# One core, two transformer blocks: indexer scores read by pairs, one pair of score matmuls moved into the first gate tile's product

## The reference, cut to what matters

```python
logits = jnp.einsum('bqhd,bsd->bqhs', qi, ik)
score = jnp.einsum('bqhs,bqh->bqs', jax.nn.relu(logits), wi)
score = jnp.where(admissible[None], score, -jnp.inf)
_, sel = lax.top_k(score, topk)
...
q = (rms_norm(bq, q_norm_g[l]) @ w_uq[l]).reshape(b, p, B_HEADS, B_HEAD_DIM)
gates = jax.nn.sigmoid((gates + b_gates[l]).astype(jnp.float32))
```

## Time and profile before

| | |
|---|---|
| median of 3 runs | 1500.18 us (1499.02 to 1501.77) |
| the profiled execution, its own time | 1499.58 us |
| its span, first to last instruction | 1497.9 us |
| PE busy | 1477.7 us, 99% of the span |
| DVE, ACT, POOL busy | 957.0, 605.1, 221.2 us |
| mean granted TensorE clock | 0.999 of full |

### The profile page before, as it was taken

One profiled execution on the slowest core, in us unless ns is written; L12 is line 12 of the kernel. 1 busy time (PEld: TensorE's weight loads), 2 busy tenths in 40 slices (PEclk: granted clock), 3 DMA queues, 4 the chain that ended last, 5 costly groups with the idle time before them and its releaser, 6 DMA issues.

```text
span 1497.9 us, 21903 instructions
## 1 busy us (share of the span) xinstructions
PE 1477.7 (99%) x8042; PEld 1233.0 (82%) x8042; DVE 957.0 (64%) x1707; ACT 605.1 (40%) x1061; POOL 221.2 (15%) x194
## 2 busy tenths in 40 slices
PE   8999999999999999999999999999999999999998
PEld 7867776878788888898898777777787888888987
DVE  6668897565795587377854372424667855873865
ACT  5235436534443243244511374444344433432434
POOL 2013324340000000000003663322400000000000
PEclk9999999999999999999999999999999999999999
DMA  7624320033333333332323202121333333333322
GB/s 174 152 65 146 117 57 1 23 104 99 98 99 99 101 97 99 98 104 71 107 85 84 56 2 85 57 64 36 102 95 99 99 99 112 89 95 98 113 70 100
DMA packets 250309, 132.99 MB, mean 89 GB/s; under 512 B 21225, under 2 KB 247653, under 8 KB 250222
## 3 DMA queue, kind: packets, MB, share of 16 engines
q1 hardware_dynamic: 247998, 123.92, 29.2%
q0 software_dynamic: 2144, 7.77, 1.8%
q10 hardware_dynamic: 80, 0.14, 0.0%
HBM read 129.67 MB, written 6.38 MB: 91 GB/s over the span
## 4 chain that ended last, share of the span: by engine, by line
PE 91%; DVE 5%; DMA 1%; issue 1%; ACT 1%; POOL 0%; SPq 0%; DVEq 0%; ACTq 0%
PE psL L2050 50%; PE psS L2073 12%; PE psL L2236 11%; PE psS L2050 5%; PE psT L2245 2%; PE psL L2371 1%; PE psS L2541 1%; PE psL L2496 1%; PE psS L2344 1%; PE psS L2519 1%; PE psS L2475 1%; DVE acc L1479 1%; PE psS L2286 1%; DVE st L1478 1%; PE psS L2476 0%
## 5 line engine op out<-in xcount | busy, mean ns | idle before, releaser
L775 ACT ACTIVATE wh<-stage 128x1024 fp32r<-128x1024 f32 (+3 forms) x232 | 225.4, 971 | 366.2 <-PE psL L2050 260.0
L2050 PE MATMUL psL<-hn,wh 128*128 128x512 f32 x1104 | 347.9, 397 | 0.4 <-DVE ft L1733 0.4
L2050 PEld LDWEIGHTS psL<-hn,wh 128*128 128x128 f32 x1104 | 204.8, 188 | 50.3 <-issue 3.7
L1208 DVE TENSOR_TENSOR wl<-stage,wh 128x1024 fp32r<-128x1024 f32 (+1 forms) x157 | 187.6, 1195 | 78.9 <-ACT wh L775 78.5
L2050 PE MATMUL psL<-hn,wl 128*128 128x512 f32 x552 | 217.1, 393 | 0.0
L2050 PE MATMUL psL<-hid,wh 128*128 128x512 f32 x680 | 209.6, 390 | 1.4 <-DVE wl L1208 1.4
L636 POOL TENSOR_TENSOR wl<-stage,wh 128x1024 fp32r<-128x1024 f32 (+2 forms) x75 | 140.0, 1867 | 278.5 <-ACT wh L775 278.5
L2236 PE MATMUL psL<-hn,wh 128*128 128x512 f32 x496 | 166.9, 418 | 2.2 <-DVE tmp L1468 2.0
L2050 PEld LDWEIGHTS psL<-hid,wh 128*128 128x128 f32 x680 | 127.4, 188 | 28.9 <-DVE wl L1208 2.2
L2050 PE MATMUL psL<-hid,wl 128*128 128x512 f32 x340 | 132.3, 389 | 0.0
L2050 PEld LDWEIGHTS psL<-hn,wl 128*128 128x128 f32 x552 | 103.8, 188 | 23.5
(11 more groups left out here) (438 smaller groups left out, 2644.3 us busy)
## 6 DMA issues: line engine op xcount, KB each, us to landing
stage<-in_w_in SPq DMA_DIRECT2D x54, 512.0 KB, 3.8
stage<-in_w_ffn_gate SPq DMA_DIRECT2D x22, 512.0 KB, 3.8
stage<-in_w_ffn_up SPq DMA_DIRECT2D x22, 512.0 KB, 3.8
stage<-in_w_ff_gate SPq DMA_DIRECT2D x22, 512.0 KB, 3.8
stage<-in_w_ff_up SPq DMA_DIRECT2D x22, 512.0 KB, 3.8
stage<-in_w_out SPq DMA_DIRECT2D x16, 512.0 KB, 4.0
stage<-in_w_ffn_down SPq DMA_DIRECT2D x16, 512.0 KB, 4.0
stage<-in_w_ff_down SPq DMA_DIRECT2D x16, 512.0 KB, 4.1
```

What stands on the lines that cost most here:

```text
L775: act.activation(wh[:, b, 0:n], stage[:, b, 0:n], ACT.Copy).then_inc(hi[b], 1)
L1208: v.tensor_tensor(wl[:, b, 0:n], stage[:, b, 0:n], wh[:, b, 0:n].bitcast(F32), ALU.subtract).then_inc(lo[b], 1)
L2050: ins = pe.matmul(dst, w[:, b, k * P:(k + 1) * P], x[:, part, k, c0:c1], start=k + n == 0, stop=k == kc - 1 and n == 2)
```

## The change

On ACT the relus are grouped by pairs: relu 9 comes ahead of `high` uq1 (1,0), relu 11 ahead of `high` gates1 (0,0), relu 13 ahead of `high` gates1 (0,1). On DVE additions 10 and 11 move by one place: addition 10 comes behind the eviction of uq1 (1,0) rather than ahead of it, addition 11 behind the eviction of uq1 (1,1). On PE `logits(6)` no longer stands between uq1 (1,1) and the gate tile; it is made inside gates1 (0,0), ahead of chunk 1. Nothing is added or removed in the arithmetic.

```diff
             relu_of(4, 8)
             high("uq1", 0, 1)
-            relu_of(8, 9)
+            relu_of(8, 10)
             high("uq1", 1, 0)
-            relu_of(9, 10)
             high("uq1", 1, 1)
-            relu_of(10, 11)
+            relu_of(10, 12)
             high("gates1", 0, 0)
-            relu_of(11, 13)
+            relu_of(12, 14)
             high("gates1", 0, 1)
-            relu_of(13, 16)
+            relu_of(14, 16)
...
             take_scaled("uq1", 0, 1, qT[:, 1, :], sq[:], QSCALE)
-            add_logits(9, 11)
+            add_logits(9, 10)
             take_scaled("uq1", 1, 0, qT[:, 2, :], sq[:], QSCALE)
+            add_logits(10, 11)
             low("gates1", 0, 0, ())
-            add_logits(11, 12)
             take_scaled("uq1", 1, 1, qT[:, 3, :], sq[:], QSCALE)
-            add_logits(12, 16)
+            add_logits(11, 16)
...
             product("uq1", 1, 1, bqg)
-            logits(6)()
...
-            product("gates1", 0, 0, hn, between={(0, 5): logits(7)})
+            product("gates1", 0, 0, hn, between={(0, 1): logits(6), (0, 5): logits(7)})
             pe.wait_ge(lg_taken, 4 * NB)
```

## The result

| | before | changed |
|---|---|---|
| median, 12 executions each | 1499.39 us | 1503.0 us (1501.06 to 1505.53) |
| the profiled execution | 1499.58 us, span 1497.9 | 1505.53 us, span 1503.8 |
| mean granted clock in it | 0.999 | 0.995 |

The ratio is 1.0019, 95% interval 1.0011 to 1.0027: slower by 2.8 us, or 1.6 to 4.0; the two medians differ by 3.6 us. The new median lies inside the predicted range of 1499.9 to 1503.8, but not at the forecast of 1501.5. That it meets rival 1's 1503.0 to the tenth is luck: rival 1 put its 2.81 us on the median of three executions, 1500.18, and over twelve the kernel before has 1499.39.

A forecast was written before the change was run, and what follows sets the result against it. PE, 99% busy, was taken as the bound, with the gate weights ending last ahead of the gate product. Pair 6 inside it (1.17) plus later weights (0.10) made 1.27 us, on the median 1500.18: 1501.5 us, range 1499.9 to 1503.8.

The forecast's parts named there:

- the forecast of 1501.5: Whole kernel: 1.27 us later at the first score of w1, put on the median of 1500.18; chance 0.47.
- rival 1: Ahead of the gate product: the 2.20 us gap drops the clock, costing 1.54 us more, 1503.0 us; chance 0.33.
- The path: Uq1 (1,0) split through gate load to gate product: later weights start the product 0.10 us later (0.03 to 0.17).
- the split's delay: POOL's `low` of uq1 (1,0), behind relu 9 on ACT: ends 0.26 to 0.40 us late, taken as 0.33.
- the lower bound: POOL's `low` of uq1 (1,0): 0.74 us long of 0.74 to 0.88, ending 0.26 us late of 0.26 to 0.40.
- The covers: POOL's later `low` of gates1 (0,1), about 2 us of cover left, and DVE's moved additions: no cost.
- the inserted pair: Pair 6 between chunks of the gate product on PE: costs 1.17 us, all on the path.
- a border between 1.34 and 2.00 us: PE gaps: whether the clock falls is decided by a gap length somewhere between these two values.
- Rival 2: At 216.67, where PE waits 2.00 us for DVE: up to all 1.27 us absorbed, 1500.2 us; chance 0.09.
- Rival 3: Ahead of the gate product: the gap closes as meant, a gain of 0.9 us, 1499.3 us; chance 0.05.

The follow-up runs named there:

- the gap filled: The changed kernel plus two extra matmuls on PE between uq1 (1,1) and the gate product, run twice: ratios to before 1.0011 and 1.0006.
- pair only: The kernel before with only pair 6 moved into the gate product, ACT and DVE as they were: ratio to before 1.0013 (1.0004 to 1.0022).
- split first: The kernel before with ACT's `high` of uq1 (1,0) put ahead of relu 8, run twice: ratios to before 0.9990 and 0.9997.
- relus only: The changed kernel with pair 6 put back ahead of the gate product: ratio to before 1.0004 (0.9994 to 1.0013).
- the second profile of the changed kernel: The unmodified changed kernel timed again beside the kernel before: ratio to before 1.0023 (1.0014 to 1.0033).
- the third changed run: The unmodified changed kernel timed a third time beside the kernel before: ratio to before 1.0021 (1.0012 to 1.0030).
- relu 9 back: The changed kernel with relu 9 back behind the split of uq1 (1,0) on ACT: ratio to before 1.0024 (1.0015 to 1.0033).
- the second filled one: Second run of the changed kernel with two extra matmuls ahead of the gate product: ratio to before 1.0006, median 1501.66 us.
- changed, split first: The changed kernel with ACT's `high` of uq1 (1,0) put ahead of relus 8 and 9: ratio to before 1.0005 (0.9995 to 1.0016).
- the first filled one: First run of the changed kernel with two extra matmuls ahead of the gate product: ratio to before 1.0011, median 1500.61 us.

## Why the prediction was right, and where it was off

**The path.** Right in kind at each step. PE idles for DVE's `low` and no longer for a relu. The landing moved by the split's delay: `high` started at 103.14 (forecast 103.0), `low` at 104.23 ended at 105.46 (105.34), PE began at 105.52 (105.38); 0.16 of this is the later start of the whole stretch. POOL's `low`, 0.88 us long before, where it ran beside DVE's addition of 97.45 to 98.09, now starts behind that addition and took 0.74, the lower bound; PE's wait grew by 0.25, the lower bound too. The load then took 3.84 us, and other executions varied by some tenths.

**The covers held.** POOL's `low` of gates1 (0,1) moved by 3.7 us, of which 1 is the clock's doing, and PE had no wait at the first quarter. DVE finished the additions at 115.50, 0.10 us behind the start of PE's first scores of w1, and still had 0.37 us to wait for them, as these rows of the changed kernel show against the earlier trace rows; POOL's, against the earlier trace rows, stands below them:

```profile
110.13 0.77 DVE L1438 SCALAR_TENSOR_TENSOR acc<-relu,iwn,acc 128x528 f32<-128x528 f32 x1
113.86 1.64 DVE L1438 SCALAR_TENSOR_TENSOR acc<-relu,iwn,acc 128x528 f32<-128x528 f32 x2 [2.96 <-ACT relu L844]
...
116.08 0.37 DVE L1484 CUSTOM_DVE_ANT_0 W3a<-psS,biasA,nsink 128x144 f32<-128x144 f32 x1 [0.37 <-PE psS L2271]
```

```profile
110.75 2.38 POOL L636 TENSOR_TENSOR wl<-stage,wh 128x1024 fp32r<-128x1024 f32 x1 [10.77 <-ACT wh L775]
```

The addition that had taken 2.50 us beside POOL takes 0.77 now, and it buys nothing: DVE idles 2.96 us right behind it.

**A term mis-sized: the inserted pair.** Forecast 1.17, measured 1.30 (8.33 - 7.03). I counted from the last start of a chunk to the first of the next and left out that the first matmuls behind the pair also follow each other more slowly. With it, the sum without the clock is 1.4: the changed kernel's product started 8.44 after relu 8, and 8.44 + 8.33 - 15.39 = 1.38, to 1.60 with the product starts of its other two executions. Forecast 1.27.

**The choice between forecast and rival 1.** This is where the forecast was wrong. The range held because it had been drawn wide enough for rival 1. All three profiled executions of the changed kernel show the fall. That it comes in most of the 36 is an estimate, since the mean clock of an execution doesn't tell where it fell. 0.61 of them ran at 0.996 or less, 0.35 with the gap filled. If each of these had the late fall of about 3 us that is described below, that makes 0.8 of the 2.1 us between the two kernels and leaves 1.3 for the fall at 106, some eight tenths of its price. It doesn't come in every one: five of the 36 ended below 1501.5 us. The price was right: 9.88 us for the product against 8.33 in "pair only" is 1.55, as forecast (1.54). Together 1.38 + 1.55 = 2.93 us, which is what the first score of w1 shows. I gave 0.33 to it although its gap of 2.20 us was longer than the one seen to lower the clock. The chances should have been the other way round. Nor is there a border between 1.34 and 2.00 us that decides, as I wrote there: gaps of 2.13 and 2.28 us kept the clock. (The gap of 2.00 us isn't the one other large one either: PE waits 2.86 and 1.29 us in its first 5 us, ahead of all products.)

**What rival 1 had wrong: a fall costs only where PE is the bound.** I took its price from the fall at 216.67, as if that one had cost the kernel 1.54 us too. The runs show that it hadn't. From that gap's end to the first `wuk` product (L2301) are 16.05 us before, and 16.09 and 15.99 in the two "split first" profiles, which fell there too. In the nine profiles that kept the clock they are 15.73 to 15.78. So this fall costs 0.3 us. Where the clock stays, PE runs into the next wait for DVE. PE's timeline in "pair only":

```profile
217.16 0.70 PE L2235 MATMUL psL<-hn,wh 128*128 128x512 f32 x2 [2.00 <-DVE tmp L1468]
...
225.34 0.70 PE L2235 MATMUL psL<-hn,wh 128*128 128x512 f32 x2 [1.09 <-DVE tmp L1468]
```

In the kernel before, with the clock down, the second wait doesn't exist; it is hidden in the slow matmuls. At 106 nothing but PE is late, and all 1.55 us count.

**Rivals 2 and 3.** Rival 2 falls: from the first score of w1 to L2301 are 120.41 us before (112.31 to 232.72) and 120.10 in the changed kernel (115.40 to 235.50), and those 0.3 are the fall above. Rival 3 falls with "relus only": the gap had another cause than the relu.

**What the profiled execution adds.** Its 5.9 us over before are more than 2.93 - 0.3. The rest, about 3 us, comes later, in two places of the span where the clock was down in it and not in before:

```profile
748.00:750.00 2.00, 2.00 (x11) 2.00 (x11) 1.66 (x11) 0.00 (x0) 0.00 (x0) 0.50 0.87 251
858.00:860.00 2.00, 2.00 (x8) 1.20 (x6) 1.51 (x5) 1.06 (x4) 1.49 (x2) 0.50 0.00 0
```

These waits of PE can serve as marks, first before, then changed:

```profile
742.62 1.95 PE L2111 MATMUL psT<-ones,sqacc 128*128 128x1 f32 x16 [0.24 <-DVE sqacc L1617]
850.87 0.71 PE L2475 MATMUL psS<-kaT,qaT 64*128 64x264 f32 x2 [0.80 <-DVE negm L1485]
745.58 1.95 PE L2110 MATMUL psT<-ones,sqacc 128*128 128x1 f32 x16 [0.24 <-DVE sqacc L1616]
854.76 0.71 PE L2473 MATMUL psS<-kaT,qaT 64*128 64x264 f32 x2 [0.80 <-DVE negm L1484]
```

The fall at 748 costs 0.9 us: between the marks are 108.25 us before and 109.18 in the changed kernel. It is in nine of the twelve profiles (109.16 to 109.20) and missing in just the three that fell at 216 (108.25 to 108.28); why it is one or the other isn't shown. The fall at 857 costs about 3.

From L2301 to the end it took 1503.8 - 235.5 = 1268.3 us, and 1500.5 - 235.2 = 1265.3 in the second profile of the changed kernel, which kept the clock there. The fall at 857 is in the profiles of the third changed run too, and of "relus only", "relu 9 back", the second filled one and "changed, split first", and not in those of before, "pair only", the first filled one and both "split first". So it comes in some executions and not in others of one kernel, and it is why two of them differ by 3 us. Whether the change makes it more frequent is open. The profiles lean that way (none of four with the old order of the relus, six of eight with the new), but the kernel before seems to have it too: the six profiles with this fall ran at a mean clock of 0.995 or 0.996 and the six without at 0.997 to 0.999, and 0.33 of before's 91 executions ran at 0.996 or less, some 2 us above its median. The difference of the means, 3.7 us over all and 3.5 within each comparison, is 0.7 or 0.6 above what the stretch explains, with errors of 0.16 and 0.26 us for the two means.

## What to carry to other kernels

A wait on the critical engine that seems to have one cause often has a second, nearly as late. Before moving work out of a gap, work out when the next item could start without it; here the gap was 1.34 us and only 0.2 of it could be had by the rows, 0.3 by the run. The pair in that gap was nearly free, and moved out of it, it cost its full 1.30. The place to gain was, by the traces, one step up the chain: a small split on ACT that fed the load of the late tile, put into idle time. Before explaining the difference of two single executions, look through the whole span for falls of the clock that one of them has and the other hasn't.

## What the runs showed of the hardware

The clock's answer to a gap isn't a fixed function of its length. In 12 profiles the same wait of 2.00 us at 215 to 220 us was followed by a fall in three (before and both "split first") and by none in nine. Ahead of the gate product, gaps of 2.26, 2.32 and 2.49 us were followed by one, gaps of 2.13 and 2.28 were not, nor were seven gaps from 0.34 to 1.60 ahead of the product or of pair 6. Nor does a fall need a gap of 2 us: the ones at 748 us came behind a wait of 0.24 us and 16 matmul passes of one column, the ones at 857 behind waits of 0.80 and 0.18 us, and with the same waits the clock stayed in three and in six of the twelve profiles. The Trainium skill, "TensorE: Matmul & The Clock Gate", section "What's actually happening", says that the hardware's observation runs freely and isn't reset when a kernel starts, so that the moment at which the clock rises varies between runs; a fall that varies in the same way would fit with it, as behind 2.26 and 2.28 us, but no run here shows the cause. Its advice on gaps, in "Why this matters for your kernels", speaks of longer ones than these; here gaps of 2.0 to 2.5 us were followed by a fall in six cases and in eleven not, and the measurement decides.

A fall isn't worth one price: 1.55 us where TensorE alone was the bound, 0.3 us where VectorE was about to make it wait anyway, 0.9 at 748 and about 3 at 857. And two useless matmuls more, 1.88 us of work for nothing, made the kernel faster by some 2 us at the mean: both profiles with them kept the clock at 106, and the three without them, of the changed kernel, did not.
